# Stick-breaking attention in a decoder block: two key blocks to a tile, and another order of ScalarE's work

## What is computed

```python
def stick_breaking_attention(q, k, v):
    """A[t,s] = sigmoid(z_ts) * prod_{s<j<t} (1 - sigmoid(z_tj)), s < t; o_t = sum_s A[t,s] v_s."""
    ...
        z = jnp.einsum('bqhd,bkhd->bhqk', qi.astype(jnp.float32), kf) * scale
        causal = key_pos[None, :] < q_pos[:, None]
        log_beta = jax.nn.log_sigmoid(z)
        log_one_minus = jnp.where(causal, jax.nn.log_sigmoid(-z), 0.0)
        suffix = lax.cumsum(log_one_minus, axis=3, reverse=True) - log_one_minus
        weights = jnp.where(causal, jnp.exp(log_beta + suffix), 0.0)
        return jnp.einsum('bhqk,bkhd->bqhd', weights, vf)
```

## Time and profile before

| | us |
|---|---|
| median of 3 runs | 9875.56 |
| lowest, highest of them | 9660.14, 10212.67 |
| the profiled execution | 9695.34 |
| its span on the slowest core | 9693.8 |
| spans of the 8 cores | 9617.6 to 9693.8 |
| busy: TensorE matmuls, VectorE, ScalarE | 7278.4, 4806.9, 4797.6 |

### The profile page before, as it was taken

The page is one execution under the profiler, slowest core; times in us unless marked ns, Lnnn a source line. Parts: engine busy times, 40 slices in busy tenths (PEclk is TensorE's granted clock), DMA queues, the critical chain, the costliest instruction groups (busy, mean ns, idle before and its releaser), DMA issues.

```text
span 9693.8 us, 131879 instructions; the slowest of 8 cores (9617.6 to 9693.8 us)
## 1 busy us (share of the span) xinstructions
PE 7278.4 (75%) x37825; PEld 3294.6 (34%) x38512; DVE 4806.9 (50%) x9010; ACT 4797.6 (49%) x9367; POOL 77.9 (1%) x107
## 2 busy tenths in 40 slices
PE   7654444677788777877788775544999995899997
PEld 7332222233233332333233232332444442444443
DVE  0225555366666665666665664443444443444444
ACT  0333333599999998999998994221111111111111
POOL 0000000000000000000000000000000000000000
PEclk9876666599999999999999997666999998999999
DMA  5430110200000000000000002224221223222211
GB/s 141 118 117 19 34 34 11 56 2 2 2 24 3 2 2 12 14 2 2 2 3 2 2 2 61 68 71 115 53 53 39 49 44 113 53 53 53 42 46 44
DMA packets 254954, 378.49 MB, mean 39 GB/s; under 512 B 90928, under 2 KB 184624, under 8 KB 253232
## 3 DMA queue, kind: packets, MB, share of 16 engines
q1 hardware_dynamic: 180544, 292.58, 9.5%
q0 software_dynamic: 73712, 77.44, 5.2%
HBM read 376.11 MB, written 71.30 MB: 46 GB/s over the span
## 4 chain that ended last, share of the span: by engine, by line
PE 54%; ACT 23%; issue 11%; DVE 8%; DMA 2%; another core or an unknown queue 1%; ACTq 1%; SPq 0%; DVEq 0%; POOL 0%; POOLq 0%
PE ps L282 50%; ACT arena L258 23%; DVE arena L269 3%; PE ps L285 2%; PE ps L280 2%; DVE arena L263 2%; DVE arena L272 1%; DVE arena L503 1%; ACTq L54 1%; DVE arena L265 1%; DMA arena<-w_inr 0%; DMA arena<-w_down 0%; SPq L111 0%; DMA out<-arena 0%
## 5 line engine op out<-in xcount | busy, mean ns | idle before, releaser
L282 PE MATMUL ps<-arena 128*128 128x512 bf16 (+5 forms) x26753 | 6795.3, 382 | 1414.5 <-ACT arena L258 870.4
L258 ACT ACTIVATE arena<-ps 128x512 bf16<-128x512 f32 (+2 forms) x5328 | 2900.1, 586 | 2921.7 <-PE ps L282 2767.7
L282 PEld LDWEIGHTS ps<-arena 128*128 128x128 bf16 (+2 forms) x27440 | 2621.7, 110 | 4729.4 <-issue 2927.3
L258 ACT ACTIVATE arena<-arena 128x512 bf16<-128x512 f32 (+9 forms) x3273 | 1916.4, 587 | 1374.7 <-DVE arena L269 465.1
L269 DVE TENSOR_TENSOR arena<-arena 128x512 f32<-128x512 f32 (+5 forms) x2800 | 1790.2, 642 | 1439.9 <-ACT arena L258 1257.1
L276 DVE CAST arena<-arena 128x512 bf16<-128x512 f32 (+3 forms) x2360 | 1018.0, 431 | 604.4 <-PE ps L280 285.5
L272 DVE SCALAR_TENSOR_TENSOR arena<-ps,arena 128x512 f32<-128x512 f32 (+1 forms) x1280 | 865.0, 685 | 285.3 <-PE ps L282 267.2
L269 DVE TENSOR_TENSOR arena<-arena,ps 128x512 bf16<-128x512 f32 x512 | 351.9, 688 | 1281.6 <-PE ps L282 1276.1
L285 PE MATMUL ps<-arena 128*128 128x128 bf16 (+1 forms) x1856 | 273.3, 322 | 947.5 <-DVE arena L263 594.0
L280 PEld LDWEIGHTS ps<-arena 128*128 128x128 bf16 x9216 | 474.9, 98 | 611.0 <-issue 518.3
L280 PE MATMUL ps<-arena 128*128 128x64 bf16 x9216 | 651.7, 193 | 3.2 <-ACT arena L258 1.1
(11 more groups left out here) (18 smaller groups left out, 196.8 us busy)
## 6 DMA issues: line engine op xcount, KB each, us to landing
arena<-w_down SPq DMA_DIRECT2D x32, 2048.0 KB, 7.5
arena<-xs SPq DMA_DIRECT2D x16, 2048.0 KB, 11.6
arena<-w_gate POOLq DMA_DIRECT2D x32, 1024.0 KB, 9.1
arena<-w_up POOLq DMA_DIRECT2D x32, 1024.0 KB, 13.0
arena<-w_ada SPq DMA_DIRECT2D x12, 2048.0 KB, 10.9
arena<-xo SPq DMA_DIRECT2D x8, 2560.0 KB, 13.5
arena<-xo SPq DMA_DIRECT2D x32, 512.0 KB, 4.4
X_s<-arena SPq DMA_DIRECT2D x32, 512.0 KB, 2.9
```

The costliest lines, as they stand in the source:

```text
L258: act.op(lambda e: e.activation(out=out_, in_=in_, func=func, **kw), reads, writes, partial=partial)
L282: pe.op(lambda e: e.matmul(out_, lhsT=lhsT, rhs=rhs, start=start, stop=stop), reads, writes, sig=sig, partial=True)
```

## The change

Two key blocks form one tile of 128 x 1024. A tile's scores lie in a pair of neighbouring PSUM banks, of which three rotate (`PSP[0]` to `PSP[2]`, t mod 3); the fourth pair holds the two AV results. ScalarE's three functions run on 1024 columns. QK is computed once: `stage2` adds its matmuls onto the scores in the same banks, after the first Exp has read them. The running sum over later tiles is used by both halves, and the second half (the lower block) takes the sum of the first by a further matmul of `onesn` with `l_t`. The cast of the running sum is made once for a tile.

ScalarE's order becomes Exp(t), second Exp of t - 2 (`stage2b`), Ln(t). Where the tile t + 3 is masked, which writes its scores to the pair that this second Exp reads, the second Exp is issued in two halves. The loop issues `stage1(it)`, `stage3(it - 3)`, `stage2(it - 1)`. There are 1152 tiles, 256 of them masked.

```diff
-        PS = [nc.alloc_psum_tensor("ps%d" % i, [128, 512], F32) for i in range(8)]
-        PSB = [p.bitcast(BF16) for p in PS]
+        PSP = [nc.alloc_psum_tensor("psp%d" % i, [128, 1024], F32) for i in range(4)]
+        PSPB = [p.bitcast(BF16) for p in PSP]
+        PS = [PSP[i // 2][:, (i % 2) * 512:(i % 2 + 1) * 512] for i in range(8)]
+        PSB = [PSPB[i // 2][:, (i % 2) * 1024:(i % 2 + 1) * 1024] for i in range(8)]
...
             def stage1(t):
+                if t >= NS:
+                    if 0 <= t - 2 < NS:
+                        stage2b(t - 2)
+                    return
                 d = steps[t]
-                u = t % 2
+                u, p3 = t % 2, t % 3
...
-                MM(PS[u][:, :], kt_ap, q_ap, True, not d["masked"], [bKTp[s_], bQTp[s_]], [bPS[u]], sig=(not d["masked"]))
-                if d["masked"]:
-                    MM(PS[u][:, :], identb, mk_ap, False, True, [bconst, bamk], [bPS[u]], sig=True)
-                ACT(e_t[u], PS[u][:, :], AF.Exp, [bPS[u]], [be[u]])
+                for half in range(2):
+                    kb = d["kb"][half]
+                    masked = kb >= 8 * d["i"]
+                    dst = pq[:, half * 512:(half + 1) * 512]
+                    MM(dst, KTp[s_][pr, kb * 128:(kb + 1) * 128], q_ap, True, not masked, [bKTp[s_], bQTp[s_]], [bPQ[p3][half]], sig=(not masked))
+                    if masked:
+                        MM(dst, identb, amk[:, (d["i"] % 2) * 8 + (kb - 8 * d["i"]), :], False, True, [bconst, bamk], [bPQ[p3][half]], sig=True)
+                ACT(e_t[u], pq[:, :], AF.Exp, bPQ[p3], [be[u]])
+                if t >= 2:
+                    stage2b(t - 2)
                 ACT(l_t[u], e_t[u], AF.Ln, [be[u]], [bl[u]], bias=1.0)
-                if d["step"] + 1 < d["nkb"]:
-                    if d["step"] == 0:
-                        CP(lsum, l_t[u], [bl[u]], [blsum])
-                    else:
-                        TT(lsum, lsum, l_t[u], ALU.add, [blsum, bl[u]], [blsum])
-                    CP(lsb[t % 3], lsum, [blsum], [blsb[t % 3]])
+                if d["tl"] == 0:
+                    CP(lsum, l_t[u][:, 0:512], [bl[u]], [blsum])
+                else:
+                    TT(lsum, lsum, l_t[u][:, 0:512], ALU.add, [blsum, bl[u]], [blsum])
+                if d["tl"] + 1 < d["nT"]:
+                    TT(lsum, lsum, l_t[u][:, 512:1024], ALU.add, [blsum, bl[u]], [blsum])
+                    CP(lsb[p3][:, 1, :], lsum, [blsum], [blsb[p3][1]])
 
             def stage2(t):
...
+                MM(pq[:, 0:512], trin, l_t[u][:, 0:512], False, d["tl"] == 0, [bconst, bl[u]], [bPQ[p3][0]], sig=False, skip=True)
+                if d["tl"] > 0:
+                    MM(pq[:, 0:512], onesn, lsb[pm][:, 1, :], False, True, [bconst, blsb[pm][1]], [bPQ[p3][0]], sig=False, skip=True)
+                MM(pq[:, 512:1024], trin, l_t[u][:, 512:1024], False, False, [bconst, bl[u]], [bPQ[p3][1]], sig=False, skip=True)
+                if d["tl"] > 0:
+                    MM(pq[:, 512:1024], onesn, lsb[pm][:, 1, :], False, False, [bconst, blsb[pm][1]], [bPQ[p3][1]], sig=False, skip=True)
+                MM(pq[:, 512:1024], onesn, l_t[u][:, 0:512], False, True, [bconst, bl[u]], [bPQ[p3][1]], sig=True, skip=True)
+
+            def stage2b(t):
+                n = t + 3
+                if n < NS and steps[n]["kb"][0] >= 8 * steps[n]["i"]:
+                    for h_ in range(2):
+                        c_ = slice(h_ * 512, (h_ + 1) * 512)
+                        ACT(a_t[t % 2][:, c_], PSP[t % 3][:, c_], AF.Exp, [bPQ[t % 3][h_]], [ba[t % 2]], partial=(h_ > 0))
+                else:
+                    ACT(a_t[t % 2], PSP[t % 3][:, :], AF.Exp, bPQ[t % 3], [ba[t % 2]])
...
-            for it in range(NS + 2):
+            for it in range(NS + 3):
                 if it < NS:
                     d = steps[it]
                     if d["pfirst"] and d["hp"] + 1 < 4:
                         pending_load = (it + 2, d["hp"] + 1)
-                    stage1(it)
+                stage1(it)
+                if 0 <= it - 3 < NS:
+                    stage3(it - 3)
                 if 0 <= it - 1 < NS:
                     stage2(it - 1)
-                if 0 <= it - 2 < NS:
-                    stage3(it - 2)
```

More of the change, by code:

```diff
@@ L612, in build_program @@
             amk = A.get(BF16, [128, 16, 512])
-            e_t = [A.get(F32, [128, 512]) for _ in range(2)]
-            l_t = [A.get(BF16, [128, 512]) for _ in range(2)]
+            e_t = [A.get(F32, [128, 1024]) for _ in range(2)]
+            l_t = [A.get(BF16, [128, 1024]) for _ in range(2)]
             lsum = A.get(F32, [128, 512])
-            lsb = [A.get(BF16, [128, 512]) for _ in range(3)]
-            a_t = [A.get(BF16, [128, 512]) for _ in range(2)]
+            lsb = [A.get(BF16, [128, 2, 512]) for _ in range(3)]
+            a_t = [A.get(BF16, [128, 1024]) for _ in range(2)]
             osb = [A.get(BF16, [128, 4, 128]) for _ in range(2)]
@@ L636, in build_program @@
                     for hh in range(2):
[L637 to L641, removed]
+                        nT = (8 * i + 8) // 2
+                        for tl in range(nT):
+                            kbA = 8 * i + 7 - 2 * tl
+                            steps.append(dict(hp=hp, s=hp % 2, i=i, hh=hh, tl=tl, nT=nT, kb=(kbA, kbA - 1),
+                                              tid=tid, osl=(hp * 8 + i) % 2, pfirst=(i == 0 and hh == 0 and tl == 0)))
@@ new lines, in stage1 @@
+            def stage1(t):
+                if t >= NS:
+                    if 0 <= t - 2 < NS:
+                        stage2b(t - 2)
+                    return
+                d = steps[t]
+                u, p3 = t % 2, t % 3
+                s_ = d["s"]
+                pq = PSP[p3]
+                pr = slice(d["hh"] * 64, (d["hh"] + 1) * 64)
+                q_ap = QTp[s_][pr, d["i"] * 512:(d["i"] + 1) * 512]
+                for half in range(2):
[8 more added lines that the diff above has]
+                    stage2b(t - 2)
+                ACT(l_t[u], e_t[u], AF.Ln, [be[u]], [bl[u]], bias=1.0)
+                if d["tl"] == 0:
[5 more added lines that the diff above has]
+                    CP(lsb[p3][:, 1, :], lsum, [blsum], [blsb[p3][1]])
@@ L669, in stage2 @@
             def stage2(t):
                 d = steps[t]
[L671 to L677, removed]
@@ L678, in stage2 @@
-                if d["step"] > 0:
-                    MM(PS[2 + u][:, :], onesn, lsb[(t - 1) % 3], False, True, [bconst, blsb[(t - 1) % 3]], [bPS[2 + u]], sig=True)
-                ACT(a_t[u], PS[2 + u][:, :], AF.Exp, [bPS[2 + u]], [ba[u]])
+                u, p3 = t % 2, t % 3
+                pq = PSP[p3]
+                pm = (t - 1) % 3
+                MM(pq[:, 0:512], trin, l_t[u][:, 0:512], False, d["tl"] == 0, [bconst, bl[u]], [bPQ[p3][0]], sig=False, skip=True)
+                if d["tl"] > 0:
+                    MM(pq[:, 0:512], onesn, lsb[pm][:, 1, :], False, True, [bconst, blsb[pm][1]], [bPQ[p3][0]], sig=False, skip=True)
@@ L686, in stage3 @@
                 ou = d["tid"] % 2
-                pso, bpso = PS[4 + ou], bPS[4 + ou]
+                pso, bpso = PS[6 + ou], bPS[6 + ou]
                 hh, osl = d["hh"], d["osl"]
[L689 to L692, removed]
+                last = d["tl"] == d["nT"] - 1
+                for half in range(2):
+                    kb = d["kb"][half]
+                    for qb in range(4):
+                        MM(pso[:, qb * 64:(qb + 1) * 64], a_t[u][:, half * 512 + qb * 128:half * 512 + (qb + 1) * 128], Vp[s_][:, kb, hh * 64:(hh + 1) * 64],
+                           (d["tl"] == 0 and half == 0 and qb == 0), (last and half == 1), [ba[u], bVp[s_]], [bpso], sig=(half == 1 and qb == 3), skip=True)
+                if last:
                     CP(osb[osl][:, :, hh * 64:(hh + 1) * 64], pso[:, 0:256].rearrange("p (a d) -> p a d", d=64), [bpso], [bosb[osl]], partial=(hh > 0))
```

13 lines of the change are left out of this document (3 added, 10 removed).

## The result

The changed kernel takes 8967.33 us (median of 13 runs, 8840.0 to 9051.53); the kernel before took 9763.82 us in the same comparison (15 runs, 9658.25 to 10212.67). The ratio is 0.9167, 95% interval 0.9114 to 0.922: the time is 8.3% shorter. The profiled execution took 8840.75 us, its span is 8839.2 us on the slowest core (core 1), the other cores' 8818.1 to 8837.3. Many executions, those of the experiments above all, held cores at a lower clock for part of the time, and the ratio leaves out those that this slowed. From here on the stage's length is read core by core, from a core's own first weight load of the stage to the end of its last AV matmul, on cores whose granted clock was 1.00 past the opening (0.96 to 0.99 in two runs, as said there). For the changed kernel it repeats within 4 us.

A forecast was written before the change was run, and what follows sets the result against it. ScalarE was taken to bound the 4119 us stick-breaking stage. 896 x 2.79 + 256 x 3.09 = 3291, + 47 opening + 45 dips = 3383 us; 736 saved from the profiled 9695.34 gives 8960 us, range 8840 to 9230.

The forecast's parts named there:

- no stall on masked tiles: Low end of the range: masked tiles wait for nothing, 2.84 us each in place of 3.09, -64 us.
- an opening and dips that shorten: Low end of the range: the stage's low-clock stretches at its start and later shrink, -55 us.
- the low clock: Stretches of the stage with TensorE at 1.2 GHz: 47 us extra in the opening, 45 in dips.
- ScalarE, width: 1024-wide instructions at 431 ns per further 512 elements: 1021, 1061, 1010 ns; width gives 0.21 us a tile.
- ScalarE, order: Second Exp of t-2 before Ln(t): 0.15 hole goes, three pairs overlap by 0.10; period 2.79 us, order gives 0.51.
- The hand-off: Second Exp of t-2 to QK(t+1) to Exp(t+1): 0.14 + 0.60 + 0.10 us, hides behind Ln with 0.02 to spare.
- Masked tiles: 256 tiles with QK and mask: 0.05 us for the cut second Exp plus a 0.25 stall, 3.09 us each.
- the useless cut: Upper bound for masked tiles: cutting the second Exp in halves gains nothing, 3.6 us a tile.
- TensorE and VectorE: Per tile TensorE needs 2.0 us and VectorE 2.32, both under ScalarE's 2.79, so neither binds.
- rival 3: TensorE sits on 1.2 GHz in the steady part and becomes the bound; whole stage so, 10365 us; chance 0.04.
- dropping the second QK: TensorE: unmasked tiles 7 matmuls of 512 for two steps' 8, masked 9 for 12; hidden behind ScalarE.
- the dropped cast: VectorE: one cast a tile fewer costs and gives nothing, hidden behind ScalarE.

The follow-up runs named there:

- the old order's run: Changed kernel, still wide with QK computed once, but ScalarE order Exp(t), Ln(t), second Exp of t - 1, never cut; stage 3496 us.
- the cut first Exp: Changed kernel with the first Exp also cut into two 512-wide halves in masked tiles; stage 3231.4 to at most 3235.2 us, fastest run 8796.73 us.
- K padded: Changed kernel with each head's K in 128 rows, the other head's 64 zero; stage 3223.5 and 3224.2 us, fastest run 8776.62 us.
- QK twice: Changed kernel with stage 2 computing QK and mask anew in the same banks; stage 3444 us on four cores, 3441 to 3455 on others.
- the narrow kernel: Changed kernel with all three ScalarE functions cut into 512-wide halves, new order kept; stage 3445.5 us on core 0.

## Why the prediction was right

The forecast was 8960 us with a stage of 3383; the profiled execution came to 8840.75 with a stage of 3285.4. The median of 8967.33 is nearer, but that is luck: it holds more than the profiled execution on which the sum is built. Against its own basis the forecast was 119 us too high, of a saving of 855, and the profiled time lies at the very low end of the stated range (8840), which had been put together otherwise: no stall on masked tiles, and an opening and dips that shorten. The stall stayed, and the low clock went almost whole. Of the 834 us that the stage lost, 771 are the pace (4044 to 3273, both without extras), which the experiments take apart; 63 are the low clock that vanished, whose cause they leave open.

- *ScalarE, width*: Exp 1030, Ln 1067, second Exp 1022 ns measured; 1021, 1061 and 1010 predicted. The 431 ns per further 512 elements of the earlier trace rows carry over from Square to the three functions; taking two PSUM banks at once costs at most the 9 to 12 ns by which the two Exp exceed the estimate.
- *ScalarE, order*: no hole ahead of Ln, and neighbours overlap also ahead of the instruction that reads SBUF, as taken from the earlier trace rows. The starts lie 0.95 apart after Ln (predicted 0.96), and 1.82 across the two Exp (predicted 0.92 + 0.91). The period is 2.77, not 2.79; on 896 tiles that is 18 us of the miss. That most of the gain is from the order holds only when it is counted first, on narrow instructions (0.52 of 0.74); with wide ones it is 0.26. The Trainium skill ("VectorE: DVE Perf Modes", section on the TRN2 errata) tells of latency exposed between instructions; here that holds for the dependent pair only, 0.15 in the old order's run, while independent neighbours overlap by 0.10.
- *The hand-off*: 0.14, 0.59 and 0.10 as read from the earlier trace rows, and it hides, with the predicted 0.02 to spare not to be told from nothing. The old order's 0.96 and the cut first Exp's 0.95 show that no time is lost there.
- *Masked tiles*: 3.09 predicted, 3.09 to 3.10 measured; a stall of 0.27 for 0.25. Both bounds that were given have shown themselves: the useless cut 3.51 (3.6 given), no stall 2.83 with K padded (2.84 given).
- *TensorE and VectorE*: TensorE waits 0.59 of 2.77 us (about 0.6 of 2.79 in rival 3), VectorE is at 61% (near 65% predicted). Neither binds in unmasked tiles. That dropping the second QK is hidden behind ScalarE is borne out for these alone; for the masked ones the sum had the nine matmuls, but never said what the second QK would cost there: 159 us in the stage. That the dropped cast gives nothing no run tests.
- *Rival 3*, TensorE at 1.2 GHz in mid-stage: 1.00 from 1804 us on. The Trainium skill ("TensorE: Matmul & The Clock Gate", section on psum-queue depth-cycling) tells of a kernel whose clock swung as it cycled through PSUM banks; with the rotation of three pairs here it didn't.
- *The term that was mis-sized is the low clock.* The sum carried 47 us for the opening and 45 for dips. 896 x 2.77 + 256 x 3.09 = 3273, so in the measured 3285.4 all such extras, the drain at the end included, are about 12. That is 80 of the 98 us by which the stage was over-estimated. The sum took over 115 us of opening at granted 0.50, the 1.2 GHz level, as if it were given in time; after, the granted clock was at 1.00 from 20 us into the stage on, and there were no dips. (By its own terms the opening passes 16 masked and 8 unmasked tiles, worth 72 us and not 68, so its 47 should have been 43.)
- *Outside the stage* 20 us are left: 9695.34 - 4119.5 = 5575.8 before, 8840.75 - 3285.4 = 5555.4 after. Core by core, span less stage is 5536 to 5574 in the profiled execution of before and 5533 to 5554 in that of the changed kernel, so this is scatter between cores, not the change.

What ended the low clock so soon isn't settled. Ahead of the stage TensorE waited idle for the loads at granted 0.50, in both kernels alike (the last 16 us ahead of 1779). From a core's first weight load on, the granted clock stayed at 0.50 for 76 to 119 us on the 8 cores of the kernel before, for 10 to 16 in the changed kernel, and never longer in its two repeats. It stayed there for 10 to 16 us on six cores and 41 on two with QK twice, for 6 to 16 with the first Exp cut, and for 3 to 8 with K padded. Windows over the opening of the changed kernel on core 1, then the first 40 us of the stage with QK twice on core 5:

```profile
1763.00:1779.00 16.00, 0.00 (x0) 0.00 (x0) 0.00 (x0) 0.00 (x0) 0.00 (x0) 0.50 0.98 211
1779.00:1799.00 20.00, 18.09 (x69) 5.15 (x69) 6.52 (x12) 13.77 (x17) 0.00 (x0) 0.69 0.89 236
1799.00:1819.00 20.00, 15.83 (x102) 6.41 (x102) 10.91 (x20) 19.14 (x27) 0.00 (x0) 1.00 0.04 17
```

```profile
1769.36:1809.36 40.00, 39.72 (x108) 10.42 (x109) 9.49 (x17) 18.86 (x24) 0.00 (x0) 0.50 0.41 113
```

The old opening had TensorE busy for 112 of 115 us and stayed at 0.50, so it was not idleness that held the clock down. Nor does less work explain the quick rise: with QK twice TensorE had hardly a gap on any core, and six of the eight rose as early as in the changed kernel. The share of 64-row matmuls, which I had suspected, is smallest where the opening is shortest (none with K padded). But with QK twice it is 4 of 13 matmuls of 512 columns in a masked tile, against 4 of 12 in the kernel before, and the openings differ all the same. No run here separates the causes that are left.

## What to carry to other kernels

Where one engine issues a chain of dependent instructions, read the starts beside the durations: the hole ahead of an instruction that reads what the one just before it wrote (0.15 us here) and the lost overlap (0.10) go when independent work is put between them, and widening and reordering share that gain. Check the ends as well, since starts can run ahead for some tiles (2.95 between starts against 2.99 in the narrow kernel). Where a wide instruction waits for several producers, cut it only in the tiles where the last producer is late: some 0.06 us of fixed cost against a stall of 0.27 or 0.75. And don't carry a slow-clock stretch of the old profile over into the sum as a fixed time; give it a range that reaches to nothing.
